# Attention heads worked off between the q and k panels of a two-stack transformer kernel

## The chip, the cores and the metric

The kernel is one launch on one core of a Trainium2 chip. The metric is the time of one execution on the device, in microseconds (us). The engines are TensorE (PE in the profile, with its weight loads as PEld), VectorE (DVE), ScalarE (ACT), GpSimd (POOL) and SyncE (SP), which issues the DMAs. Each engine works off its own list of instructions strictly in order, and a wait on a semaphore holds up everything behind it on that engine.

## The reference

The input is a stream of 256 tokens of width 1024. Two layers of a first stack, each with a convolutional feed-forward network (FFN) of inner width 2816, are followed by a second, larger block (a state-space branch, two attention-like branches and a mixture of 32 experts), whose norms are modulated by a vector that comes out of a small product with the "ada" weights. The change touches only the second layer of the first stack and its neighbours:

```
h = rms_norm(x, odd_norm_g)
q, k, v = split(h @ w_qkv)            # 16 heads of 64
q, k = rotary(q), rotary(k)
o = dilated_attention(q, k, v)        # 3 patterns, softmax over their log-sum-exps
x = x + o @ w_o
x = x + (silu(gate) * val) @ w_down   # the second FFN, gate and val from conv(rms_norm(x) @ w_up)
```

With 256 tokens the attention comes down to two blocks of 128 queries: for a head, 128 queries against 128 keys and 128 queries against 256 keys, with a bias that holds the mask and the weights of the patterns; then exp, a division by the sum, and the product with v.

## The kernel before, in words

Activations lie transposed, features on partitions and tokens along the free axis (128x256 tiles). Weights come in panels of 128x1024 f32 (512 KB) through a ring of four slots. In the first stack a panel is split into a rounded part `w_hi` (ACT, L1210 and L1216) and a remainder `w_lo` (DVE at L1559; GpSimd at L1530 for every fourth panel, slot 3), and one product is three matmuls: w_hi with r_hi (L598), w_hi with r_lo (L599), w_lo with r_hi (L600). A panel of eight input tiles is thus 24 matmuls into one of the four PSUM banks `lin[b]`. SyncE reloads a slot once it is split, so panels are loaded and split up to four ahead; ACT takes the rounded part of panel n+4 right after it took the result of panel n.

The second layer runs like this.

**Projection to q, k and v.** PE goes through 24 panels: q (8), k (8), v (8). After each of the 16 q and k panels ACT copies the result to `qs1` (L1255), and PE multiplies it by a permutation that swaps the halves of a head (`swap_halves`, L799, one matmul that goes in after the next panel). DVE multiplies by cos (L1759), the swapped one by sin (L1761), adds the two (L1762) and then makes `w_lo` of a later panel. The v panels are only copied.

**Attention.** After all 24 panels PE transposes v (16 transposes, L815, in four groups of which DVE copies each, L1769). Then a loop over 16 heads, skewed over the engines: in step i PE makes the scores of head i (L826, L827, into one half of `mixp`), after every second head one eighth of the third modulation row (L732), transposes the probabilities of head i-2 (L837, into one of two banks of `stat`), and multiplies the transposed probabilities of head i-3 by v (L846 to L848). DVE reads the scores and adds the bias (L1778), takes the maxima (L1782), and for the head before takes reciprocals (L1787) and scales (L1789); every second step it splits the output of a pair of heads into r_hi and r_lo (L1576, L1577). ACT makes exp (L1352) and copies the transposed probabilities (L1360):

```
if g >= 2:
    pe.wait_ge(pt_copied, g - 1)      # before the transposes of head g
```

**Behind it.** PE waits for the last pair of heads (`o_copied`), turns the modulation row into columns (`modulation_columns`, L741), waits until DVE has read them (`mod_read`), and goes on with the 8 panels of the output projection and with the FFN. The first FFN has two such groups of columns turned in the middle of its down projection.

**DMA order.** SyncE issues three ada loads of 1 MB ahead of the 24 panels, and the last five behind the fourth panel of the output projection; the ring for ada has three slots, so load a waits until PE has used row a-3 (L494), and the other four panels of the projection are queued behind these loads:

```
load_panels(3 * KD)
load_panels(4)
load_ada(5)
load_panels(KD - 4)
```

Of the kernel before, what the change touches and what calls it, by code (L numbers as in the profile page):

```python
# [29 lines left out]
P = 128  # L30
T = 256
# [147 lines left out]
def program(nc, A, out):  # L179
# [3 lines left out]
    with ctx:  # L183
# [263 lines left out]

        def downbank(n):

            return statbank(n) if n < 2 else mixbank(n)  # L450
# [119 lines left out]
        def _(pe):  # L570
# [99 lines left out]
            def ffn(modulated=False):  # L670
# [14 lines left out]
                if modulated:  # L685
                    pe.wait_ge(modrow_ready, 2)
# [15 lines left out]
                if modulated:  # L702
# [87 lines left out]
            ffn(True)  # L790


            def swap_halves(n):

                b = (qk_first + n) % 4
                pe.wait_ge(bank_free[b], panels.free[b])
                if n >= 2:
                    pe.wait_ge(qk_ready, n - 1)
                pe.matmul(stat[:, 2 * (n % 2), :], K["swap"], qs1[:, n % 2, :], start=True, stop=True)\  # L799
                    .then_inc(rot_ready, 1)  # L800

            qk_first = panels.n
            for n in range(16):
                linear(None, 1, first=n == 0)
                if n:
                    swap_halves(n - 1)
            linear(None, 1)
            swap_halves(15)
            linear(None, 7)
            panels.settled()  # L810
            for g in range(4):
# [6 lines left out]
            pe.wait_ge(vt1_copied, 4)  # L818
            pe.wait_ge(qk_ready, 16)
            for i in range(HEADS + 3):  # L820
                if i < HEADS:
# [7 lines left out]
                if i < HEADS and i % 2 == 1:  # L829
                    modulation(lin[2], 16 + i // 2, 1)  # L830
                if 2 <= i <= HEADS + 1:
                    g = i - 2
                    pe.wait_ge(probs_ready, g + 1)
                    if g >= 2:
                        pe.wait_ge(pt_copied, g - 1)
                    for c in range(3):
                        mm = pe.transpose(statbank(g)[:, c * P:(c + 1) * P], p1[:, g % 4, c * P:(c + 1) * P], K["ident"])  # L837
                    mm.then_inc(pt_ready, 1)
                if i >= 3:
                    g = i - 3  # L840
                    pe.wait_ge(pt_copied, g + 1)
                    if g >= 4 and g % 2 == 0:
                        pe.wait_ge(o_copied, g // 2 - 1)
                    o = lin[(g // 2) % 2][64 * (g % 2):64 * (g % 2) + 64, :]
# [5 lines left out]
            pe.wait_ge(o_copied, 8)  # L850
            modulation_columns(lin[2], 2)
            pe.wait_ge(mod_read, 3)
            project(None)
            ffn()
# [337 lines left out]
        def _(act):  # L1192
# [147 lines left out]
            for n in range(16):  # L1340
                if n >= 2:
                    act.wait_ge(qk_ready, n - 1)
                take(qs1[:, n % 2, :])
            for n in range(8):
                take(v1[:, n, :])
            for i in range(HEADS + 2):
                if i < HEADS:
# [7 lines left out]
                if i >= 2:  # L1355
# [4 lines left out]
                    act.activation(pt1[:, g % 4, :], statbank(g)[:, 0:SC], ACT.Copy).then_inc(pt_copied, 1)  # L1360
                    if i == HEADS:
                        split_hi(OUT1 + 1)
# [172 lines left out]
        def _(dve):  # L1535
# [61 lines left out]
            def ffn(l):  # L1597
# [57 lines left out]
                if l == 0:  # L1655
                    modulations(lin[0], 0)
                    modulations(lin[1], 1)
                for b in range(4):
# [97 lines left out]
            for n in range(16):  # L1756
                panels.taken(0)
                panels.advance(1)
                link(dve.tensor_tensor(rc1[:, 0, :], qs1[:, n % 2, :], K["cos"], ALU.mult))  # L1759
                dve.wait_ge(rot_ready, n + 1)  # L1760
# [501 lines left out]
```

## Time and profile before

| | us |
|---|---|
| median of 3 runs | 1676.15 (1671.21 to 1681.73) |
| profiled execution | 1676.46 |
| its span | 1674.7 |

| engine | busy, share of the span |
|---|---|
| PE | 1555.6 (93%) |
| PEld | 1269.1 (76%) |
| DVE | 691.7 (41%) |
| ACT | 511.4 (31%) |
| POOL | 117.7 (7%) |

The profiled execution is 0.3 us above the median. A busy time adds the time in which an engine had at least one instruction of its own under way. The ends of matmuls are modelled, so that PE is better read from the distance of the starts of two matmuls than from their lengths. In the timelines a row gives the start, the length, the engine, the line and the tiles; x8 is a number of instructions merged into a row; what stands in brackets is the idle time before it and what ended it. Two records with one line and one length next to each other belong to one f32 matmul, which PE takes in two.

### The profile page before, as it was taken

Reading aid. Unit: us, or ns where it says so; the run is one execution under the profiler, and the core shown is the slowest. Engines: PE = TensorE matmul, PEld = TensorE weight load, DVE = VectorE, ACT = ScalarE, POOL = GpSimd, SP = SyncE. Lnnn points to the kernel's source line nnn. Section 1 sums busy time; section 2 is a strip of 40 time slices with the busy share of each in tenths; the row PEclk is TensorE's granted clock in tenths of the full one; section 3 lists DMA queues with packets and bytes.
Section 4 is the critical chain, followed back from the end, with each engine's and each line's share of the span. In section 5 each row is a group of like instructions: output and inputs, shape, how many; then the busy total and the mean of one; then the engine's idle time right before and its main releaser. Section 6 shows DMA issues by size and latency. Waiting matters only on the chain.

```text
span 1674.7 us, 26947 instructions
## 1 busy us (share of the span) xinstructions
PE 1555.6 (93%) x10672; PEld 1269.1 (76%) x10672; DVE 691.7 (41%) x1296; ACT 511.4 (31%) x831; POOL 117.7 (7%) x50
## 2 busy tenths in 40 slices
PE   7988999989998999989998887998899999999997
PEld 5767999989678999978887876887666655555554
DVE  5945888357566886232414421412311111111111
ACT  2355554354446564352223104202111101111100
POOL 0111122212001122100000000000000000000000
PEclk9989999999999999989999987999799999999999
DMA  7664555745434656514442211354799999999994
GB/s 298 235 261 164 168 168 165 254 137 166 146 115 125 188 182 184 161 50 146 131 126 76 64 38 50 105 155 139 298 428 426 427 428 426 428 425 428 427 427 208
DMA packets 57977, 375.72 MB, mean 224 GB/s; under 512 B 6560, under 2 KB 6816, under 8 KB 42272
## 3 DMA queue, kind: packets, MB, share of 16 engines
q1 hardware_dynamic: 57888, 374.43, 60.6%
q8 instruction: 69, 1.13, 0.3%
q14 instruction: 20, 0.16, 0.0%
HBM read 373.35 MB, written 1.05 MB: 224 GB/s over the span
## 4 chain that ended last, share of the span: by engine, by line
PE 62%; DMA 15%; issue 12%; DVE 6%; ACT 3%; POOL 0%; SPq 0%; POOLq 0%; DVEq 0%; ACTq 0%
PE lin L617 15%; DMA moe_arena<-in_experts 14%; PE lin L598 5%; PE mixp L1145 4%; PE lin L599 4%; PE lin L600 4%; PE mixp L1149 4%; DVE mixers L1700 3%; PE lin L901 2%; PE stat L1169 2%; PE lin L1124 1%; PE stat L598 1%; PE mixp L600 1%; PE mixp L598 1%; PE stat L600 1%
## 5 line engine op out<-in xcount | busy, mean ns | idle before, releaser
L598 PE MATMUL lin<-r_hi,w_hi 128*128 128x256 f32 x1024 | 301.4, 294 | 16.8 <-DVE r_lo L1571 8.9
L599 PE MATMUL lin<-r_lo,w_hi 128*128 128x256 f32 x1024 | 293.7, 287 | 0.0
L600 PE MATMUL lin<-r_hi,w_lo 128*128 128x256 f32 x1024 | 293.6, 287 | 0.0
L617 PE MATMUL lin<-h,ring 128*128 128x256 f32 x1280 | 288.0, 385 | 3.0 <-DVE h L1583 3.0
L617 PEld LDWEIGHTS lin<-h,ring 128*128 128x128 f32 x1280 | 245.8, 193 | 40.7 <-issue 6.9
L598 PEld LDWEIGHTS lin<-r_hi,w_hi 128*128 128x128 f32 x1024 | 200.3, 196 | 22.9 <-issue 9.6
L599 PEld LDWEIGHTS lin<-r_lo,w_hi 128*128 128x128 f32 x1024 | 200.9, 196 | 0.7
L600 PEld LDWEIGHTS lin<-r_hi,w_lo 128*128 128x128 f32 x1024 | 200.5, 196 | 0.0
L1559 DVE TENSOR_TENSOR w_lo<-ring,w_hi 128x1024 fp32r<-128x1024 f32 x126 | 156.0, 1242 | 93.6 <-ACT w_hi L1216 70.1
L2175 DVE TENSOR_TENSOR moe_arena<-moe_arena,mixp 128x256 f32<-128x256 f32 x32 | 13.5, 421 | 353.3 <-ACT moe_arena L1505 353.3
L1216 ACT ACTIVATE w_hi<-ring 128x1024 fp32r<-128x1024 f32 x124 | 130.0, 1050 | 59.8 <-PE mixp L600 54.5
L1530 POOL TENSOR_TENSOR w_lo<-ring,w_hi 128x1024 fp32r<-128x1024 f32 x42 | 106.7, 2541 | 495.7 <-ACT w_hi L1216 299.3
L1169 PE MATMUL stat<-moe_arena 128*64 128x512 f32 x512 | 116.9, 598 | 0.0
L1145 PE MATMUL mixp<-moe_arena,h 128*64 128x256 f32 x512 | 77.6, 381 | 10.8 <-DMA moe_arena<-in_experts 10.8
L1145 PE MATMUL mixp<-moe_arena,cat 128*64 128x256 f32 x512 | 77.7, 381 | 5.2 <-DMA moe_arena<-in_experts 4.3
L1505 ACT ACTIVATE moe_arena<-mixp 128x256 f32<-128x256 f32 x32 | 12.3, 384 | 221.5 <-PE mixp L1149 221.5
L1169 PEld LDWEIGHTS stat<-moe_arena 128*64 128x64 f32 x512 | 33.9, 136 | 59.1 <-issue 54.8
L1149 PE MATMUL mixp<-moe_arena,cat 128*64 128x256 f32 x512 | 77.2, 379 | 0.0
L1149 PE MATMUL mixp<-moe_arena,h 128*64 128x256 f32 x512 | 77.0, 379 | 0.0
L1124 PE MATMUL lin<-moe_arena 64*128 64x256 f32 x528 | 65.9, 389 | 1.4 <-ACT moe_arena L1509 1.4
L1145 PEld LDWEIGHTS mixp<-moe_arena,h 128*64 128x64 f32 x512 | 35.7, 137 | 39.8 <-DMA moe_arena<-in_experts 21.3
L1262 ACT ACTIVATE ub<-lin,colp 128x256 f32<-128x256 f32 x88 | 49.3, 560 | 47.8 <-PE lin L600 47.8
(378 smaller groups left out, 2332.3 us busy)
## 6 DMA issues: line engine op xcount, KB each, us to landing
moe_arena<-in_experts SPq DMA_DIRECT2D x96, 2048.0 KB, 18.5
ring<-in_panels SPq DMA_DIRECT2D x272, 512.0 KB, 3.6
aring<-in_ada SPq DMA_DIRECT2D x24, 1024.0 KB, 6.3
cst<-in_consts SPq DMA_DIRECT2D x1, 1696.0 KB, 11.7
x<-in_x SPq DMA_DIRECT2D x1, 1024.0 KB, 4.7
out_x<-x SPq DMA_DIRECT2D x2, 512.0 KB, 2.6
mixers<-in_even_w_s SPq DMA_DIRECT2D x1, 512.0 KB, 13.4
colp<-in_cols SPq DMA_DIRECT2D x1, 361.5 KB, 5.1
```

The lines of the kernel that those rows point to most:

```text
L598: pe.matmul(o, w_hi[:, slot, c], r[0], start=start, stop=False, skip_group_check=True)
L599: pe.matmul(o, w_hi[:, slot, c], r[1], start=False, stop=False, skip_group_check=True)
L600: return pe.matmul(o, w_lo[:, slot, c], r[0], start=False, stop=stop, skip_group_check=True)
L617: mm = pe.matmul(lin[b][:, 0:T], w[:, i, :], rhs[:, i, :], start=i == 0, stop=i == k - 1)
L1124: mm = pe.matmul(lin[m // 2][:, (m % 2) * T:(m % 2 + 1) * T], e_yb[64 * half:64 * half + 64, j * P:(j + 1) * P], e_dT[64 * half:64 * half ...
L1145: pe.matmul(o[:, 0:T], lhs, e_wg[:, slot, k, half * T:(half + 1) * T], start=k == 0, stop=k == KD - 1, skip_group_check=True)
L1149: mm = pe.matmul(o[:, T:2 * T], lhs, e_wu[:, slot, k, half * T:(half + 1) * T], start=False, stop=k == KD - 1, skip_group_check=True)
L1169: mm = pe.matmul(statbank(1)[64 * half:64 * half + 64, :], e_hidT[:, k % 2, k // 2, :], e_wd[:, slot, k, half * 512:(half + 1) * 512], sta ...
L1216: act.activation(w_hi[:, n % RING, :], ring[:, n % RING, :], ACT.Copy).then_inc(w_hi_ready, 1)
L1530: pool.tensor_tensor(w_lo[:, POOL_SLOT, :], ring[:, POOL_SLOT, :], w_hi[:, POOL_SLOT, :].bitcast(F32), ALU.subtract).then_inc(w_split_pool, 1)
L1559: dve.tensor_tensor(w_lo[:, n % RING, :], ring[:, n % RING, :], w_hi[:, n % RING, :].bitcast(F32), ALU.subtract)\
L1700: ins = dve.scalar_tensor_tensor(cv0[:, j, :], hc0[:, j, tap:tap + T], w, cv0[:, j, :], ALU.mult, ALU.add)
```

## The change

1. The order of the panels in the weight stream is v (8), then q0, k0, q1, k1, ... (16).
2. PE projects v, then q0; transposes two groups of v; projects k0; transposes the other two. From then on each panel is followed by the swap of the panel before it and by one step of the head loop: `head(2n-3)` after panel 2n, `head(2n-2)` after panel 2n+1. Steps up to 12 go between panels. Steps 13 to 18 come behind the last panel.
3. The swapped product lies in the second half of the panel's own bank `lin[b]`; the transposed probabilities have one bank only (`statbank(0)`), so the transposes of head g wait for the copy of head g-1; the outputs of the heads lie in `stat[:, 2:4]`.
4. All eight parts of the modulation row stand behind the last panel: one after each of steps 13 to 18, two behind step 18. PE then waits for ACT's copy of the row (`modrow_ready`) and for all r_lo (`r_split`) ahead of the output projection.
5. The head outputs are copied to `h` by DVE; from the 13th step on ACT rounds them (`round_heads`) and DVE takes the remainder (`lower_heads`), instead of both by DVE out of PSUM at once.
6. The columns of the third group are turned within the down projection of the second FFN, and DVE reads them there.

```diff
-            def ffn(modulated=False):
+            def ffn(chunks):
...
-                if modulated:
-                    for chunk in range(2):
-                        pe.wait_ge(bank_free[chunk], panels.free[chunk])
-                        modulation_columns(lin[chunk], chunk)
+                for chunk in chunks:
+                    pe.wait_ge(bank_free[chunk], panels.free[chunk])
+                    modulation_columns(lin[chunk], chunk)
...
+            linear(None, KD, first=True)
+            v_taken, qk_first = list(panels.free), panels.n
+
+            def qk_panel(m):
+
+                if m >= 4:
+                    pe.wait_ge(qk_ready, m - 3)
+                linear(None, 1)
+
+            def swap_halves(m):
+
+                b = (qk_first + m) % 4
+                pe.wait_ge(bank_free[b], v_taken[b] + m // 4 + 1)
+                pe.matmul(swapped(b), K["swap"], qs1[:, m % 2, :], start=True, stop=True, skip_group_check=True)\
                     .then_inc(rot_ready, 1)
...
-            pe.wait_ge(vt1_copied, 4)
-            pe.wait_ge(qk_ready, 16)
-            for i in range(HEADS + 3):
-                if i < HEADS:
+            def head(i):
+
+                if 0 <= i < HEADS:
+                    pe.wait_ge(qk_ready, 2 * (i // 2) + 2)
+                    pe.wait_ge(vt1_copied, 4)
...
-                if i < HEADS and i % 2 == 1:
-                    modulation(lin[2], 16 + i // 2, 1)
...
-                    if g >= 2:
-                        pe.wait_ge(pt_copied, g - 1)
+                    if g:
+                        pe.wait_ge(pt_copied, g)
...
+            for n in range(8):
+                qk_panel(2 * n)
+                if n:
+                    swap_halves(2 * n - 1)
+                    head(2 * n - 3)
+                else:
+                    turn_values(0)
+                    turn_values(1)
+                qk_panel(2 * n + 1)
+                swap_halves(2 * n)
+                if n:
+                    head(2 * n - 2)
+                else:
+                    turn_values(2)
+                    turn_values(3)
+            swap_halves(15)
+            pe.wait_ge(qk_ready, 15)
+            panels.settled()
+            for i in range(13, HEADS + 3):
+                head(i)
+                modulation(lin[2], 16 + (i - 13), 1)
+            modulation(lin[2], 22, 2)
+            pe.wait_ge(modrow_ready, 3)
+            pe.wait_ge(r_split, 1 + KH + KD)
             project(None)
-            ffn()
+            ffn((2,))
...
# ACT
+            for n in range(8):
+                take_qk(2 * n)
+                if n:
+                    head(2 * n - 3)
+                take_qk(2 * n + 1)
+                if n:
+                    head(2 * n - 2)
+            def round_heads(first, last):
+
+                act.wait_ge(panel_done, panels.n)
+                for j in range(first, last):
+                    act.wait_ge(o_copied, j + 1)
+                    act.activation(r_hi[:, j, :], h[:, j, :], ACT.Copy).then_inc(r_hi_ready, 1)
+
+            for i in range(13, HEADS + 2):
+                head(i)
+                round_heads(max(i - 11, 0) if i > 13 else 0, i - 10)
+            round_heads(7, KD)
...
# DVE
-                    split_rows(j, lin[j % 2][:, 0:T]).then_inc(o_copied, 1)
+                    dve.tensor_copy(h[:, j, :], headbank(j)).then_inc(o_copied, 1)
...
+            for n in range(8):
+                if n:
+                    rotate(2 * n - 1)
+                    head(2 * n - 3)
...
+                rotate(2 * n)
+                if n:
+                    head(2 * n - 2)
+            rotate(15)
+            def lower_heads(first, last):
+
+                for j in range(first, last):
+                    dve.wait_ge(r_hi_ready, seen(r_hi_ready))
+                    dve.tensor_tensor(r_lo[:, j, :], h[:, j, :], r_hi[:, j, :].bitcast(F32), ALU.subtract).then_inc(r_split, 1)
+
+            for i in range(13, HEADS + 3):
+                head(i)
+                if i >= 14:
+                    lower_heads(i - 12 if i > 14 else 0, i - 11)
+            split_lo(OUT1 + 2)
+            lower_heads(7, KD)
```

`rotate(m)` on DVE is what the loop over n did before for a panel: cos, sin, add, and `w_lo` of the panel four on. `take_qk(m)` on ACT is the copy of a panel's result and `w_hi` of the panel four on.

## Rows read from the trace of the kernel before

**Rows 1.** The page: busy time, share of the span and instructions of each engine.

```profile
PE 1555.6 (93%) x10672; PEld 1269.1 (76%) x10672; DVE 691.7 (41%) x1296; ACT 511.4 (31%) x831; POOL 117.7 (7%) x50
```

**Rows 2.** Windows: stretch, its length, busy time of each engine, PEclk, DMA share, GB/s.

```profile
353.90:432.77 78.87, 78.78 (x608) 77.65 (x608) 52.97 (x77) 34.76 (x54) 17.49 (x6) 0.96 0.48 148
432.77:484.39 51.62, 46.23 (x297) 26.99 (x297) 40.27 (x121) 23.78 (x83) 0.00 (x0) 0.97 0.34 116
441.00:443.00 2.00, 2.00 (x10) 0.79 (x12) 1.82 (x7) 1.24 (x5) 0.00 (x0) 0.64 0.86 365
443.00:446.00 3.00, 3.00 (x18) 1.28 (x11) 1.28 (x6) 1.60 (x6) 0.00 (x0) 0.67 0.20 36
```

**Rows 3.** Timeline of PE: first transposes of v, first transposes of probabilities.

```profile
433.20 1.06 PE L815 MATMUL mixp<-cst,mixers 128*128 128x128 f32 x8 [0.52 <-issue]
440.67 0.55 PE L837 MATMUL stat<-cst,mixers 128*128 128x128 f32 x3 [1.24 <-DVE mixers L1789]
```

**Rows 4.** Timeline of PE: parts of the head loop and one ada part.

```profile
462.44 0.55 PE L837 MATMUL stat<-cst,mixers 128*128 128x128 f32 x3
462.92 0.43 PE L846 MATMUL lin<-mixers 128*64 128x128 f32 x2
463.72 0.48 PE L826 MATMUL mixp<-mixers 64*128 64x128 f32 x2
464.57 1.07 PE L732 MATMUL lin<-aring,c_act 128*32 128x512 f32 x8
465.57 0.55 PE L837 MATMUL stat<-cst,mixers 128*128 128x128 f32 x3
```

**Rows 5.** Timeline of PE, two groups of columns amid the first FFN's down projection.

```profile
332.80 1.84 PE L741 MATMUL lin<-cst,modrow 128*128 128x4 f32 x16
334.50 0.36 PE L598 MATMUL stat<-hid_hi,w_hi 128*128 128x256 f32 x1
```

**Rows 6.** Timeline of PE: first matmul of the output projection, two later ones.

```profile
484.39 0.39 PE L598 MATMUL lin<-r_hi,w_hi 128*128 128x256 f32 x1 [1.30 <-DVE mod L1672]
487.20 0.41 PE L598 MATMUL lin<-r_hi,w_hi 128*128 128x256 f32 x1
487.41 0.41 PE L599 MATMUL lin<-r_lo,w_hi 128*128 128x256 f32 x1
```

**Rows 7.** Timeline of PE, a swap between two panels.

```profile
411.95 0.59 PE L799 MATMUL stat<-mixers,cst 128*128 128x256 f32 x2
412.49 0.28 PE L599 MATMUL lin<-r_lo,w_hi 128*128 128x256 f32 x1
```

**Rows 8.** w_lo by DVE, whole kernel: count, ns min/median/max.

```profile
L1559 DVE TENSOR_TENSOR w_lo<-ring,w_hi x126: 1210/1222/3471, 112.9 to 697.4; 128x1024 fp32r<-128x1024 f32 x126
```

**Rows 9.** Timeline of DVE and ACT in one step of the head loop.

```profile
462.55 0.56 DVE L1778 SCALAR_TENSOR_TENSOR mixers<-mixp,cst 128x384 f32<-128x384 f32 x1 [0.82 <-PE mixp L827]
463.14 0.61 DVE L1782 TENSOR_REDUCE mixers<-mixers 128x1 f32<-128x128 f32 x2
463.79 0.40 ACT L1352 ACTIVATE mixers<-mixers 128x128 f32<-128x128 f32 x1 [1.33 <-DVE mixers L1782]
463.87 0.55 DVE L1789 TENSOR_SCALAR mixers<-mixers 128x128 f32<-128x128 f32 x2
464.33 0.42 DVE L1576 CAST r_hi<-lin 128x256 fp32r<-128x256 f32 x1
464.69 0.47 ACT L1360 ACTIVATE mixers<-stat 128x384 f32<-128x384 f32 x1
```

**Rows 10.** DMA issues in 433 to 485: count, size, median us to landing.

```profile
aring<-in_ada SPq DMA_DIRECT2D x5, 1024.0 KB, 5.0
```

**Rows 11.** Timeline of ACT, the copy of the modulation row.

```profile
480.03 0.59 ACT L1308 ACTIVATE modrow<-lin 128x512 f32<-128x512 f32 x1
```

**Rows 12.** Timeline of POOL and DVE, w_lo of two panels beside each other.

```profile
364.05 2.40 POOL L1530 TENSOR_TENSOR w_lo<-ring,w_hi 128x1024 fp32r<-128x1024 f32 x1 [19.92 <-ACT w_hi L1210]
364.06 3.47 DVE L1559 TENSOR_TENSOR w_lo<-ring,w_hi 128x1024 fp32r<-128x1024 f32 x1
```

More of the change, by code:

```diff
@@ L789, in _, with turn_values @@
             modulation(mixbank(1), 11, 5)
[L790 to L799, printed above, removed]
-                    .then_inc(rot_ready, 1)
[L802 to L811, printed above, removed]
+            ffn((0, 1))
+            linear(None, KD, first=True)
[8 more added lines that the diff above has]
+                pe.matmul(swapped(b), K["swap"], qs1[:, m % 2, :], start=True, stop=True, skip_group_check=True)\
+                    .then_inc(rot_ready, 1)
+            def turn_values(g):
+                for b in range(4):
+                    pe.wait_ge(bank_free[b], v_taken[b])
                 if g >= 2:
@@ L1339, in _, with take_qk, head @@
             stream_norm(down=True)
[L1340 to L1343, printed above, removed]
             for n in range(8):
                 take(v1[:, n, :])
-            for i in range(HEADS + 2):
-                if i < HEADS:
+            def take_qk(m):
+                if m >= 2:
+                    act.wait_ge(qk_ready, m - 1)
+                take(qs1[:, m % 2, :])
+            def head(i):
+                if 0 <= i < HEADS:
                     act.wait_ge(max_ready, i + 1)
@@ L1755, in _ @@
             split_lo(panels.n + 4)
[L1756 to L1760, printed above, removed]
-                link(dve.tensor_tensor(rc1[:, 1, :], stat[:, 2 * (n % 2), :], K["sin"], ALU.mult))
-                dve.tensor_tensor(qk1[:, n, :], rc1[:, 0, :], rc1[:, 1, :], ALU.add).then_inc(qk_ready, 1)
-                dve.wait_ge(qk_ready, n + 1)
-                split_lo(panels.n + 4)
-            panels.advance(8)
-            split_lo(panels.n)
-            for g in range(4):
-                dve.wait_ge(vt1_ready, g + 1)
-                dve.tensor_copy(vt1[:, g // 2, (g % 2) * 512:(g % 2 + 1) * 512], mixbank(g)).then_inc(vt1_copied, 1)
+            panels.advance(KD)
+            qk_first = panels.n
             a0 = list(K).index("bias00")
@@ L1772, in _, with rotate, head @@
             bias = cst[:, bias_at:bias_at + SC]
-            for i in range(HEADS + 3):
-                if i < HEADS:
+            def rotate(m):
+                panels.taken(0)
+                panels.advance(1)
+                link(dve.tensor_tensor(rc1[:, 0, :], qs1[:, m % 2, :], K["cos"], ALU.mult))
+                dve.wait_ge(rot_ready, m + 1)
+                link(dve.tensor_tensor(rc1[:, 1, :], swapped((qk_first + m) % 4), K["sin"], ALU.mult))
+                dve.tensor_tensor(qk1[:, 8 * (m % 2) + m // 2, :], rc1[:, 0, :], rc1[:, 1, :], ALU.add).then_inc(qk_ready, 1)
+                dve.wait_ge(qk_ready, m + 1)
+                split_lo(panels.n + 4)
+            def head(i):
+                if 0 <= i < HEADS:
                     dve.wait_ge(scores_ready, i + 1)
```

45 lines of the change are left out of this document (25 added, 20 removed).

## The prediction

> **What bounds the kernel now.** I read the page first: PE is busy 93% of the span, DVE 41%, ACT 31% [rows 1]. So work that leaves DVE or ACT is worth nothing by itself; only time in which PE stands still, or runs at a lower clock, can be won. Next I cut out the stretch that the change rearranges, with the windows [rows 2]: from the first matmul of the q, k, v projection at 353.90 to the first of the output projection at 484.39, 130.49 us in two parts. In the first part, 78.87 us, PE is busy for 78.78: nothing to win. The second part, the attention, is 51.62 us. The timeline tells what of it is PE's own work. Eight transposes of v take 1.06 [rows 3], 16 take 2.1. A step of the head loop, start to start, is 0.48 for the transposes, 0.80 for the product with v and 0.85 for the scores, 2.13 together; an ada part between steps adds 464.57 to 465.57, 1.00 [rows 4]. There the parts follow each other with no gap, so in mid-loop PE is the bound in the attention too. The sum is 2.1 + 16 x 2.13 + 8 x 1.00 + 0.85 for the columns (half of 332.80 to 334.50 [rows 5]) = 45.0. So 6.6 us of 51.62 is lost: waits like 0.52 and 1.24 [rows 3] and 1.30 [rows 6], and 5 us at a granted clock of 0.64 and 0.67 [rows 2], which is 2 x 0.36 + 3 x 0.33 = 1.7 us. **6.6 us, or 0.4% of the kernel, is the most that the rearrangement can win** in this stretch; the change takes no matmul away.
>
> **Part 1, panels reordered, v first.** The same 24 panels, swaps, w_hi and w_lo. The panels of the weight stream change places, not size or number. 0 (bounds 0 and 0: 78.78 of 78.87 was busy, and v panels need only a copy).
>
> **Part 2, heads between panels.** Steps up to 12 move between panels. I play one half period, from the end of a panel at 0. A panel is 24 matmuls at 0.12, 2.9 us; a swap put between panels costs 412.49 - 411.95 - 0.12 = 0.42 [rows 7]; a step 2.13; together 5.4 us for PE. PE: swap at 0, scores done at 1.2, transposes and product with v done at 2.5, next panel until 5.4, next swap and scores until 6.6, then the next transposes. DVE: sin and add, two 128x256 operations like the cast of 0.42, until 1.4; w_lo 1.22 [rows 8] until 2.6; read of the scores 0.59 until 3.2; maxima 0.53 until 3.7 (0.73 with the reciprocal, 0.2, taken off); reciprocal and scale 0.7 until 4.4; copy of an output until 4.9 [rows 9]. ACT: exp 0.90 from 3.8 to 4.7, copy of the transposed probabilities 0.47 until 5.2 [rows 9]. The next transposes want this copy, as there is one bank for them now, and PE is there at 6.6. The copy is 1.4 us early, the scaled probabilities 2.2. The cover for this is the panel of 2.9 us; without it PE would wait 1.5 us a step. So no wait between panels. What is added is a change of matmul kind: swap and head stand together, and the swap's 0.42 holds the change back to w_hi already, so another change costs between 0 and 0.42 for each of 13 insertions, nearer to 0; I take 0.09, **+1.2 us** (0 to 5.5).
>
> **Part 3, what is left behind the last panel.** Steps 13 to 18 have no panel to hide behind, only an ada part of 1.0 each. The clock starts at the end of the last panel. PE: step 12 until 2.5, last swap 2.8, scores of 13 at 3.6. The copy it needs is that of step 12, 5.2 by the schedule above: **waits 1.7**. Transposes, product, ada part until 7.6, scores of 14 at 8.5. DVE meanwhile: step 12 until 4.9, cos, sin, add until 6.2, w_lo until 7.4, read and maxima of 13 until 8.5; ACT exp and copy until 10.0: PE **waits 1.5**. Step 14 with its ada part ends at 12.4, scores of 15 at 13.2. ACT rounds three outputs until 11.3 and is done with step 14 at 12.7. DVE, held by the remainders of three outputs (3 x 0.42), has the maxima of 15 at 14.4, ACT's copy is at 15.9, and PE, done with step 15 at 15.5, **waits 0.5**. The rest goes at PE's pace: step 16 ends at 18.3, 17 at 20.6, 18 at 22.4.
>
> Then the ada rows. Before, the eight parts were 5 us apart; now they stand 2 to 5 us apart with two at the end. The ring holds three, so the load of part 22 is issued when PE is done with 19 (18.3), that of 23 when it is done with 20 (20.6). Landing takes 5.0 us [rows 10]: 23.3 and 25.6. PE is there at 22.4 and 24.3: **waits 0.9 and 1.3**, and ends at 26.6. Then ACT copies the row, 0.59 [rows 11], with 0.2 around it, and PE, now told to wait for it, **waits 0.8**: the output projection starts at 27.4. On SyncE the last four panels of the projection are queued behind these loads, as before; they are issued at 20.6, and PE wants the first of them four panels after 27.4. Nobody is late by that.
>
> Waits: 1.7 + 1.5 + 0.5 + 0.9 + 1.3 + 0.8 = 6.7 us. The granted clock fell once before, behind the waits at the start of the head loop, for 1.7 us; the same kind of waits stand at the start of this tail, so I take 1.7 again (0 to 3.4: never, or twice). Both together 8.4, against 6.6 before: **+1.8 us**. The low end, with the waits of the tail gone, is -6.6; the high end, with each wait twice as long, +8.5.
>
> **Part 4, modulation columns.** Out of the stretch come 0.85 of work (its waits are in the 6.6). They reappear within the down projection of the second FFN for 0.85 and a change of kind: net 0 to 0.2. DVE's reads there have a whole down projection beside them: 0. The projection's first matmuls ran at 0.21 apart around 487.20 instead of 0.12 [rows 6]; the wait ahead of it stays of like size, so this stays.
>
> **Part 5, outputs through h.** The operations on the outputs go from two on DVE to two on DVE and one on ACT, off PE's path except for the 0.5 above.
>
> **Sum.** 0 + 1.2 + 1.8 + 0.1 = +3.1 us on the profiled execution of 1676.46, which stands 0.3 above the median of 1676.15: 1679.3 from the median, **1679 us**. A measurement of this kernel can hardly tell less than 1% (17 us) from no change; its three runs lie 10 us apart. This is no change.
>
> **Rivals.**
>
> *The handover works.* If ACT and DVE keep ahead in the tail, because they have caught up during the last panel more than I count, and the ada loads land in time, the waits and the lower clock of the tail go: 3.1 - 8.4 = -5.3, 1671 us. For it: before, the loop ran at PE's pace with the same chain. Against it: there the transposes had two banks, and DVE now starts the tail with a rotation and a w_lo in front.
>
> *GpSimd holds DVE.* At 364.05 a w_lo on GpSimd of 2.40 us ran beside one on DVE that took 3.47 instead of 1.22, 2.25 more [rows 12]. In the panels with heads there are three of GpSimd's (behind the 6th, 10th and 14th q or k panel). Were DVE held for 2.25 right behind the scores, the copy would come 2.25 - 1.4 = 0.9 late: 3 x 0.9 = 2.7, 1682 us. It decides nothing near 1%. Against it: of that half period DVE does not make a w_lo itself. The Trainium skill (SBUF — State Buffer, "Who interferes with whom") calls the port pair of VectorE and GpSimd an exclusive lock, which whoever starts first has for a whole instruction. That agrees with the row of 3.47. By that rule the read of the scores, with one operand in PSUM, would go on beside GpSimd, and only the scale would be held; the scale has 2.2 us to spare by the schedule above, and this rival would cost nothing.
>
> *The clock falls between the panels* (the other side). The panels' stretch was granted 0.96 with only a 128x256 swap between panels; the heads' small matmuls and their waits brought stretches at 0.64 and 0.67 [rows 2]. At the lower clock of 1.2 GHz matmuls stand 0.21 instead of 0.12 apart [rows 6], so a panel costs 24 x 0.09 = 2.2 us more. Fourteen panels have heads about them: 14 x 2.2 = 30, 1710 us; from seven panels on (3 + 15) it is more than 1%. For it: the heads leave PE's array partly unused. Against it: in mid-loop the heads alone, with no wait, ran at full clock, and my schedule has no wait between the panels.
>
> *The order convoys*, so that each inserted step waits a little for DVE or ACT: half a us for each of 13 is 6.5, 1686 us. It would need the 1.4 us of slack above to be used up first.
>
> **How the numbers follow.** The forecast 0.58; the handover works 0.20; GpSimd 0.05; convoy 0.08; clock 0.07; something that speeds the kernel by over 1% 0.02, which no row offers: 6.6 us of lost time bound it. The low end of the range is the handover case, 1671; the high end takes in the convoy, 1688. Left out are the clock case and the tails of the others. Faster by over 1%: 0.02. Slower by over 1%: the clock case and a bit of a worse convoy, 0.08. Within 1%: 0.90.
>
> **What would show it.** PE without a gap between panels, a half period of 5.4 us, and the copy of the transposed probabilities over a us ahead of the next transposes; behind the last panel waits of one to two us on ACT's copies in steps 13 and 14, then on the ada DMAs of parts 22 and 23 (not there: the landing was faster, or the steps slower); 27 us from the end of the last panel to the output projection; 133 us for the whole stretch; four column matmuls within the second down projection. Wrong would be gaps between the panels, a granted clock under 0.9 there, or a tail under 20 us.

## The result, and the profile after

The changed kernel took 1686.49 us in the median of 7 runs (1680.71 to 1689.46), the kernel before 1676.64 (1671.19 to 1681.73): ratio 1.0063, 95% interval 1.0042 to 1.0084. It is slower by 0.4 to 0.8%, so within 1%, and 7.5 us above the time forecast. The profiled execution took 1686.49, its span is 1684.7, 10.0 above that of before. In the rows of the changed kernel L812 is the swap, L835 the scores, L844 the transposes, L853 the product with v, L738 an ada part, L747 the columns and L606 to L608 the three matmuls of a panel.

The windows cut the span of the changed kernel where those of before were cut: the part with the panels, what stands behind the last panel, and the stages between the end of the second FFN and the first expert load. Columns as in [rows 2].

```profile
354.03:461.00 106.97, 106.97 (x769) 94.47 (x769) 73.70 (x154) 51.37 (x113) 17.28 (x6) 0.97 0.35 109
461.00:488.23 27.23, 20.47 (x128) 8.70 (x127) 14.03 (x43) 9.46 (x31) 0.00 (x0) 0.89 0.67 249
...
711.21:1173.69 462.48, 423.25 (x2144) 371.71 (x2142) 140.88 (x243) 116.08 (x187) 0.00 (x0) 0.93 0.31 91
```

The stretch of [rows 2] was 130.49 us and is 134.20: +3.7. PE is busy for all of 106.97 in the panels' part, with heads between the panels, and for 20.47 of 27.23 behind it. From there to the end of the second FFN it was 222.03 and is 222.98, +0.95. The stages behind, which no line of the change touches, were this before:

```profile
706.42:1163.68 457.26, 417.65 (x2144) 366.80 (x2142) 140.81 (x243) 116.10 (x187) 0.00 (x0) 0.95 0.31 92
```

The same 2144 matmuls, DVE busy for 140.8 and ACT for 116.1 in both, yet 5.2 us more and a granted clock of 0.93 instead of 0.95. So of 10 us that the profile shows, 4.7 lie where the change is, and 5.2 where it is not. Neither figure is free of the clock: in the first ten microseconds of the output projection, for one, it was 0.78 here and 0.83 before.

**Between the panels**, the timeline of PE shows one half period, from swap to swap:

```profile
435.31 0.59 PE L812 MATMUL lin<-mixers,cst 128*128 128x256 f32 x2
435.83 0.48 PE L835 MATMUL mixp<-mixers 64*128 64x128 f32 x2
436.68 0.55 PE L844 MATMUL stat<-cst,mixers 128*128 128x128 f32 x3
437.16 0.43 PE L853 MATMUL stat<-mixers 128*64 128x128 f32 x2
...
440.93 0.59 PE L812 MATMUL lin<-mixers,cst 128*128 128x256 f32 x2
```

No row carries a bracket, so nothing was waited for. The parts of a step stand 0.85 and 0.48 apart as in [rows 4], but the period is 5.62, where a panel with a swap (24 x 0.12 + 0.42) and a step (2.13) make 5.43. The swap takes 0.52 until the scores. The copies that the transposes need were early, as forecast: the one before the transposes of 442.31 ends at 440.67, 1.6 us ahead. GpSimd held DVE there, at no cost to PE: beside its w_lo the scale took 1.39 us instead of 0.55:

```profile
425.72 3.45 POOL L1580 TENSOR_TENSOR w_lo<-ring,w_hi 128x1024 fp32r<-128x1024 f32 x1 [18.06 <-ACT w_hi L1239]
428.13 1.39 DVE L1847 TENSOR_SCALAR mixers<-mixers 128x128 f32<-128x128 f32 x2
```

**Behind the last panel** (the swap after it starts at 457.80), the timeline of PE at each wait:

```profile
463.30 0.52 PE L844 MATMUL stat<-cst,mixers 128*128 128x128 f32 x3 [1.30 <-ACT mixers L1393]
467.91 0.52 PE L844 MATMUL stat<-cst,mixers 128*128 128x128 f32 x3 [1.45 <-ACT mixers L1393]
475.44 0.52 PE L844 MATMUL stat<-cst,mixers 128*128 128x128 f32 x3 [0.51 <-ACT mixers L1393]
482.64 1.06 PE L738 MATMUL lin<-aring,c_act 128*32 128x512 f32 x8 [0.82 <-DMA aring<-in_ada]
485.68 1.86 PE L738 MATMUL lin<-aring,c_act 128*32 128x512 f32 x8 [1.98 <-DMA aring<-in_ada]
488.23 0.58 PE L606 MATMUL lin<-r_hi,w_hi 128*128 128x256 f32 x1 [0.70 <-ACT modrow L1337]
```

Three waits for ACT's copy of transposed probabilities, two for the last ada loads, one for the copy of the row: 6.8 us. The row of 485.68 lasts 1.86 instead of 1.07 [rows 4]: the lower clock. From the end of the last panel to the output projection it is 30.4 us, where the schedule had 27.4 and the clock's 1.7 beside it.

What stands ahead of ACT's copies is seen in the timeline of DVE and ACT:

```profile
462.69 0.47 ACT L1393 ACTIVATE mixers<-stat 128x384 f32<-128x384 f32 x1
464.03 1.22 DVE L1609 TENSOR_TENSOR w_lo<-ring,w_hi 128x1024 fp32r<-128x1024 f32 x1
465.18 0.55 DVE L1836 SCALAR_TENSOR_TENSOR mixers<-mixp,cst 128x384 f32<-128x384 f32 x1
466.41 0.40 ACT L1385 ACTIVATE mixers<-mixers 128x128 f32<-128x128 f32 x1 [3.25 <-DVE mixers L1840]
467.30 0.47 ACT L1393 ACTIVATE mixers<-stat 128x384 f32<-128x384 f32 x1
```

The scores of step 13 were done by 462.0, but DVE rotates the last panel and makes a w_lo first, reads them at 465.18, and ACT, idle for 3.25, comes to the copy at 467.30, for which PE waits until 467.91.

**In the second FFN** the columns stand where they were put, and 703.67 - 702.87 = 0.80 goes to them (with the change of kind behind them 0.9):

```profile
702.87 0.95 PE L747 MATMUL lin<-cst,modrow 128*128 128x4 f32 x8
703.67 0.36 PE L606 MATMUL stat<-hid_hi,w_hi 128*128 128x256 f32 x1
```

### The profile page after: what moved, and what is told of

It is laid out like the page before. It is cut to its first block, busy times and chain, and to the rows that moved or that the text cites. A ratio compares the mean times of both kernels' runs of the same rounds, so it can differ in the third digit from the quotient of the medians.

```text
span 1684.7 us, 26972 instructions
## 1 busy us (share of the span) xinstructions
PE 1564.5 (93%) x10672; PEld 1273.2 (76%) x10672; DVE 692.8 (41%) x1296; ACT 512.3 (30%) x839; POOL 117.4 (7%) x50
## 3 DMA queue, kind: packets, MB, share of 16 engines
HBM read 373.35 MB, written 1.05 MB: 222 GB/s over the span
## 4 chain that ended last, share of the span: by engine, by line
PE 62%; DMA 15%; issue 12%; DVE 6%; ACT 4%; POOL 0%; SPq 0%; POOLq 0%; DVEq 0%; ACTq 0%
PE lin L625 14%; DMA moe_arena<-in_experts 14%; PE lin L606 5%; PE mixp L1174 4%; PE lin L607 4%; PE lin L608 4%; PE mixp L1178 4%; DVE mixers L1757 3%; PE lin L930 2%; PE stat L1198 2%; PE lin L1153 1%; PE stat L606 1%; PE mixp L608 1%; PE mixp L606 1%; PE stat L607 1%
## 5 line engine op out<-in xcount | busy, mean ns | idle before, releaser
L606 PE MATMUL lin<-r_hi,w_hi 128*128 128x256 f32 x1024 | 300.0, 293 | 16.3 <-DVE r_lo L1621 8.9
L608 PE MATMUL lin<-r_hi,w_lo 128*128 128x256 f32 x1024 | 293.2, 286 | 0.0
L606 PEld LDWEIGHTS lin<-r_hi,w_hi 128*128 128x128 f32 x1024 | 200.0, 195 | 25.8 <-issue 11.8
L608 PEld LDWEIGHTS lin<-r_hi,w_lo 128*128 128x128 f32 x1024 | 200.6, 196 | 0.0
L1153 PEld LDWEIGHTS lin<-moe_arena 64*128 64x128 f32 x528 | 48.4, 186 | 18.6 <-issue 12.3
```

The lines of the kernel that those rows point to most:

```text
L606: pe.matmul(o, w_hi[:, slot, c], r[0], start=start, stop=False, skip_group_check=True)
L608: return pe.matmul(o, w_lo[:, slot, c], r[0], start=False, stop=stop, skip_group_check=True)
L1153: mm = pe.matmul(lin[m // 2][:, (m % 2) * T:(m % 2 + 1) * T], e_yb[64 * half:64 * half + 64, j * P:(j + 1) * P], e_dT[64 * half:64 * half ...
```

## The experiments

Medians and ratios are against runs of the kernel before on the same chip. Its median was 1678.28 in the first series (18 runs), 1678.71 in the second (35) and 1676.33 in the third (17). The first series has before_late_5, before_late_2, tail_fill and columns_back, the second before_again, after_again, before_columns and tail_best, the third the other four; before and after are the runs of the result.

| kernel | median | ratio (95%) | stretch | to the end of FFN 2 | stages behind |
|---|---|---|---|---|---|
| before | 1676.64 | 1 | 130.49 | 222.03 | 457.26 |
| before_again | 1678.66 | 1.0005 (0.9988, 1.0023) | 130.56 | 219.76 | 459.63 |
| before_columns | 1675.66 | 0.9994 (0.9978, 1.0009) | 128.23 | 220.47 | 461.34 |
| before_late_2 | 1682.37 | 1.0030 (1.0009, 1.0052) | 130.46 | 224.66 | 461.39 |
| before_late_5 | 1688.08 | 1.0064 (1.0046, 1.0082) | 134.96 | 229.74 | 461.58 |
| before_late_5_again | 1686.10 | 1.0051 (1.0031, 1.0072) | 130.63 | 228.22 | 461.52 |
| before_late_7 | 1692.58 | 1.0076 (1.0049, 1.0103) | 134.98 | 233.21 | 458.26 |
| after | 1686.49 | 1.0063 (1.0042, 1.0084) | 134.20 | 222.98 | 462.48 |
| after_again | 1686.79 | 1.0047 (1.0029, 1.0065) | 134.13 | 223.13 | 462.54 |
| columns_back | 1684.52 | 1.0044 (1.0028, 1.0060) | 136.78 | 222.68 | 456.97 |
| after_late_2 | 1689.31 | 1.0065 (1.0044, 1.0086) | 134.92 | 226.85 | 457.13 |
| tail_fill | 1682.13 | 1.0039 (1.0011, 1.0067) | 131.03 | 220.47 | 458.08 |
| tail_best | 1675.39 | 0.9990 (0.9976, 1.0005) | 126.1 | 223.5 | 458.55 |
| tail_best_2 | 1674.79 | 0.9985 (0.9974, 0.9997) | 125.2 | 222.7 | 457.38 |

The last three columns come from the one profile of each kernel: from the first q, k, v matmul to the first of the output projection, from there to the first residual addition behind the second FFN, from there to the first expert load. The last two kernels have 2 us of ada work behind the start of the projection.

### A shift by other means

```diff
+                if not modulated:
+                    pe.wait_ge(bank_free[2], panels.free[2])
+                    for r in range(6):
+                        for i in range(4):
+                            pe.matmul(lin[2][:, 4 * i:4 * i + 4], modrow[:, 0, i * P:(i + 1) * P], K["ident"][:, 0:P:32],
+                                      start=True, stop=True, skip_group_check=True)
                 for k in range(18, KF - 2):
```

> The kernel before, with six groups of four column matmuls without use (0.85 us a group) put into the down projection of the second FFN: 5.1 us of PE work more, ahead of the stages that neither kernel changes. Theory A (clock episodes move with the program): the stages from the end of the second FFN to the first expert load were 457.2 us before and 462.4 after the change, with the same instructions, because all of them start 4.8 us later and the stretches at the lower clock fall on other work; a shift of 5.1 by other means then gives 462 too, and the total is up 10 (1687). Theory B (the changed program itself slows these stages): they stay at 457 and the total is up 5 (1682).

> The same with three groups, 2.55 us. Theory A: the later stages take anything from 455 to 463 us, not in proportion to the shift. Theory B: 457, and the total is up 2.5.

 (The edit with 3 rounds instead of 6.)

The medians rose by 10 and 4. Taken alone they speak for theory A. But the profile of before_late_5 lost 4.5 us already in the head loop, 250 us ahead of the first added instruction:

```profile
452.20 1.94 PE L738 MATMUL lin<-aring,c_act 128*32 128x512 f32 x8
...
434.00:456.00 22.00, 19.63 (x90) 10.20 (x89) 13.19 (x39) 7.65 (x28) 0.00 (x0) 0.69 0.31 103
```

The same window of before, with the same instructions in the same order:

```profile
434.00:456.00 22.00, 19.63 (x121) 10.26 (x120) 16.84 (x52) 9.09 (x35) 0.00 (x0) 0.92 0.41 144
```

PE was busy for 19.63 us in both and started 121 matmuls in one and 90 in the other. The granted clock fell behind the same wait, and came back after less than 5 us in the one (0.64 over two microseconds and 0.67 over three [rows 2]) and after some 14 in the other, where ada parts took 1.94 instead of 1.07 as late as 452.20. That is no effect of the program, which is the same up to there: here the drop begins behind the same wait, but its length is drawn anew in each execution.

And the probe is not clean. The second FFN took 7.7 us more than before for what was meant as 5.1 us of added work. The 24 column matmuls stand from 702.91 to 708.91, which is 6.0; the clock fell within them and stayed down behind them:

```profile
706.00:716.00 10.00, 10.00 (x61) 10.00 (x62) 0.00 (x0) 0.00 (x0) 0.59 (x1) 0.66 0.17 56
```

### The clock: is the loss behind the second FFN drawn or caused?

> The kernel before, unchanged, once more. Theory A in its second form (the lower clock comes and goes in time of its own, and how much of each disturbed stage it takes is drawn anew in each execution): this profile has the same instructions in the same order, yet the stages from the end of the second FFN to the first expert load may take anything from 457 to 462.5 us and the head loop 51 to 56; its times spread over 10 us and its median is the one of before. Rival (the lower clock is a fixed function of the program): the profile repeats that of before within 0.5 us in each stage, 130.5, 222.0, 457.3.

> The changed kernel, unchanged, once more. What the change itself costs is then the difference of medians over many runs: by the two stretches it touches 3.7 + 0.95 = 4.7 us, ratio 1.003, if the 5.2 us behind the second FFN were drawn (theory A, second form); 10 us, ratio 1.006, if they belong to the change. The stretch to the output projection repeats at 132 to 136 us by either.

Neither kernel has an edit. The windows behind the second FFN, of before_again:

```profile
703.15:1162.78 459.63, 420.05 (x2144) 369.47 (x2142) 140.87 (x243) 115.99 (x187) 0.00 (x0) 0.94 0.30 92
```

and of after_again:

```profile
711.63:1174.17 462.54, 423.31 (x2144) 371.71 (x2142) 140.82 (x243) 116.03 (x187) 0.00 (x0) 0.93 0.30 91
```

The fixed function is out: before_again has 2.4 us more here than before, and 2.3 less in the stage ahead, where the output projection ran without the drop of [rows 6], as the first ten microseconds of that stage show, of before:

```profile
484.39:494.50 10.11, 10.11 (x72) 10.11 (x73) 2.38 (x5) 2.73 (x4) 0.67 (x1) 0.83 0.53 183
```

and of before_again:

```profile
483.39:493.50 10.11, 10.11 (x82) 10.06 (x83) 2.71 (x6) 3.46 (x6) 1.98 (x1) 1.00 0.56 192
```

Over all fourteen profiles these stages took 457.0 to 462.5 us with the same matmuls; in the nine read this way a longer one has a lower granted clock, 0.95 at 457 and 0.93 from 461 on. The Trainium skill (TensorE: Matmul & The Clock Gate, "What's actually happening") says that the gate looks at activity on a beat that does not start with the kernel, so that the same kernel comes out differently from run to run; the two windows of the head loop above agree in that: the same instructions, 0.92 and 0.69.

Where the 5.2 us arise can be read by setting the two profiles against each other, instruction for instruction. Counted from the start of these stages, the changed kernel is 1.6 us behind after 35 us and 5.2 behind from DVE's instruction at 990.4 on (1000.4 in the changed kernel), and most of the 3.6 between comes in the few microseconds ahead of it. One instruction of PE there, before, and the next of its line:

```profile
984.44 1.09 PE L1020 MATMUL mixp<-arena 128*64 128x128 f32 x8 [0.85 <-DVE arena L2022]
991.55 1.97 PE L1020 MATMUL mixp<-arena 128*64 128x128 f32 x8 [1.30 <-DVE arena L2019]
```

and the first of them in the changed kernel:

```profile
990.83 1.86 PE L1049 MATMUL mixp<-arena 128*64 128x128 f32 x8 [0.85 <-DVE arena L2099]
```

The wait ahead is 0.85 us in both. Before, the clock was still up behind it and fell two waits later; in the changed kernel it fell behind this one. That is no effect of the change, since before_again, with no edit, has the early drop too (1.80 us for that row, at 979.80). So in a row of waits it is also drawn at which of them a drop begins.

But the changed kernel had 462.5 twice, and its ratio 1.0047 (1.0029 to 1.0065) over 12 more runs is 4.9 to 10.9 us, which leaves out 4.7, though barely. So chance alone does not cover it.

The granted clock that each run has on record tells more than two profiles. Its mean is 0.9611 over the 19 runs of the changed kernel and 0.9644 over 82 runs of before from the three series, 0.0033 less, give or take 0.0011 (95%); within the second series alone it is 0.9612 (12 runs) against 0.9643 (35). So the changed kernel does run at a lower clock on average. Over those 82 runs an execution is 1.1 us shorter for each 0.001 that its clock is higher. By that estimate 3.7 us of the 8.4 between the means of the two kernels are the clock's, and 4.7, give or take 1, are there at an equal clock. In tail_best and tail_best_2 below, which differ from the changed kernel in the tail and the first two panels behind it alone, the mean clock is 0.9657 and 0.9666 (12 runs each): it is the order of the tail that costs the clock. Some of it falls in the tail itself; how much falls in later stages, and why, is open.

Three more kernels asked whether the time follows a beat in the shift:

> The kernel before, with eight groups of useless column matmuls in the second FFN, 6.8 us. So far a shift of 2.55 cost 5 us in the median and one of 5.1 cost 10.7 (7.7 to 13.7). If the lower clock follows a beat of its own, against which the shift moves the later stages, the cost beyond the shift is not in proportion: at 6.8 it may be back to nothing, total 7 to 9, less than at 5.1. If a shift simply costs double (each us late costs another), the total is 13.6. If the excess was chance, 6.8.

> The shift of 5.1 once more on the same chip as the one of 6.8. Beat: again 8 to 11 us over before. Chance: 5.1, with the stages behind the second FFN anywhere from 457 to 462.5 in the profile.

> The changed kernel, with three groups of useless column matmuls in the second FFN, 2.55 us. Two profiles of the changed kernel had 462.5 us behind the second FFN; the one with the columns back, which gets there 2.2 us later, had 457.0. Beat: 2.55 us later than the changed kernel, these stages take 457 to 459, and the total is 2 to 3 us under the changed kernel though it does more. Chance or a cost of the program itself: 2.5 over it, 1689.

```diff
+                if 2 in chunks:
+                    pe.wait_ge(bank_free[3], panels.free[3])
+                    for r in range(3):
+                        for i in range(4):
+                            pe.matmul(lin[3][:, 4 * i:4 * i + 4], modrow[:, 0, i * P:(i + 1) * P], K["ident"][:, 0:P:32],
...
```

The beat's forecasts missed, but for the repeat of 5.1 (8 to 11 us, 9.8 came): 6.8 us of work cost 1.0076 (8 to 17 us) and was not back to nothing, and after_late_2 was 2.8 us above the changed kernel, not 2 to 3 under it, though its profile had the short form of the later stages, 457.13. Forecast of a price of double was 13.6 for the 6.8, and 12.7 came; but most of the double price is the probe's own: in the profiles 5.1 us of added work made the FFN 7.7 and 6.2 longer, 6.8 made it 11.2. With that, the ratios of the shifted kernels hold no excess that is clear of their intervals. What stays is this: in a single profile up to 5.5 us of the later stages are drawn, so the repeated 462.5 proves nothing by itself; that the changed kernel has the lower clock on average is shown by its 19 runs, and a beat in the shift, of which two of three forecasts missed, does not explain it.

### Part 4 alone, and undone

```diff
-            modulation_columns(lin[2], 2)
-            pe.wait_ge(mod_read, 3)
+            pe.wait_ge(modrow_ready, 3)
             project(None)
-            ffn()
+            ffn((2,))
...
```

> The kernel before with part 4 of the change alone: the third group of columns is turned amid the second FFN. Out of the stretch go 0.85 us of matmuls and waits of up to 1.3, into the FFN come 0.95: the stretch 128.2, the FFN 223, the sum 1.2 us shorter. By medians hardly to be told from before. If the columns' new place cost more than that, the FFN would be above 223.5.

The stretch came to 128.23, forecast 128.2. The stage to the end of the second FFN came to 220.47, not 223: in this profile, as in before_again, the output projection started at full clock (1.00 over its first ten microseconds). Against before_again the two stages together are 1.6 us shorter, forecast 1.2. The ratio, 0.9994 (0.9978 to 1.0009), cannot tell a gain of that size.

```diff
-            pe.wait_ge(modrow_ready, 3)
+            modulation_columns(lin[2], 2)
+            pe.wait_ge(mod_read, 3)
             pe.wait_ge(r_split, 1 + KH + KD)
             project(None)
-            ffn((2,))
+            ffn(())
...
```

> The changed kernel with part 4 undone: the third group of columns is turned right ahead of the output projection again, which waits for DVE's reading. Both theories of the stretch: the projection starts 0.85 for the matmuls and 1.3 for the wait later, 2.2 us, and the second FFN is 0.95 shorter; so the end of the second FFN comes 1.2 us later than in the changed kernel. Theory A for the stages behind: anything from 455 to 463 us. Theory B: 462, as in the changed kernel.

The stretch grew by 2.6, forecast 2.2, and the end of the second FFN came at 713.40, 2.2 later than in the changed kernel, forecast 1.2: the drop behind the last ada wait now also covers the columns, 1.87 instead of 1.05. Behind it the profile is among the short ones (456.97), so that this span is 3.5 us shorter than the changed kernel's with the same work in it. The ratios of the two kernels, 1.0044 and 1.0047, have intervals that overlap. Moving the columns is right and by the profiles worth one to two microseconds; it is not the loss.

### The tail: filled, then rearranged

```diff
+                if i >= 13:
+                    modulation(lin[2], 16 + (i - 13), 1)
                 if 2 <= i <= HEADS + 1:
...
                 head(i)
-                modulation(lin[2], 16 + (i - 13), 1)
```

> The changed kernel, with the ada part of each of the steps 13 to 18 put between the scores and the transposes of the step instead of behind it, so that it covers the wait for ACT's copy. Theory (the tail is a chain of waits that PE sits out): waits of 1.3 and 1.45 us in steps 13 and 14 fall by up to 1.0 each, that of 0.5 in step 16 goes; the loads of the last ada parts are issued that much earlier; the stretch to the output projection falls from 134.2 to about 131, to 129 if the granted clock stays up. Rival (the tail is bound by the DVE and ACT chain): the waits stay in sum and the stretch stays within 0.7 us of 134.2.

The waits of PE in the tail, in total, times, longest:

```profile
PE lin L738 <- DMA aring<-in_ada: 3.3, 3, 1.4
PE stat L846 <- ACT mixers L1394: 1.8, 2, 1.5
PE lin L606 <- ACT modrow L1338: 0.7, 1, 0.7
```

The stretch was 131.03; forecast was 131, and 129 if the clock stayed up. It did stay up, 1.00 behind the panels, so by that the time came out 2 us too long. The waits for ACT fell from 3.3 to 1.8; that for the loads rose from 2.8 to 3.3, since the parts now follow each other faster than loads of 5 us land in a ring of three. The wait of 1.45 in step 14, forecast to fall by up to 1.0, did not move at all.

```diff
-            modulation(lin[2], 22, 2)
-            pe.wait_ge(modrow_ready, 3)
             pe.wait_ge(r_split, 1 + KH + KD)
-            project(None)
+            for m in range(KD):
+                if m == 2:
+                    pe.wait_ge(modrow_ready, 3)
+                linear(None, 1)
+                if m == 0:
+                    modulation(lin[0], 22, 2)
+                if m >= 2:
+                    stream_sum([m - 2])
+            for m in (KD - 2, KD - 1):
+                stream_sum([m])
```

Beside this the ada parts of steps 13 to 18 stand between scores and transposes, as in tail_fill, and all eight go into the bank lin[0].

> The changed kernel, with the ada part of steps 13 to 18 between scores and transposes, in bank lin[0] instead of lin[2], and the last two parts behind the first panel of the output projection instead of ahead of it; PE waits for the copy of the row only ahead of the third panel. Theory (the last waits on ada loads and on the row's copy are exposed for their place alone): in the last kernel 1.03 and 1.42 for loads and 0.7 for the copy go; the output projection starts at about 127 us of the stretch, with 2 us of ada work behind it; from the first q, k, v matmul to the end of the second FFN 349 us against 357 of the changed kernel and 352.5 before; the median 3 us under before. Rival (the time is lost in the panels' part, by 0.2 us a step): the tail gains nothing that the median shows, and this kernel stays 3 us or more above before.

The projection starts at 479.71, 126.1 us from the start of the stretch, with no wait for a load or the row:

```profile
PE stat L846 <- ACT mixers L1401: 1.8, 2, 1.5
PE lin L606 <- DVE r_lo L1880: 1.5, 1, 1.5
```

To the end of the second FFN it is 349.7, against 357.2 in the changed kernel, 352.5 before and 350.3 in before_again. The median fell by 11 us from that of after_again, taken on the same chip, of which these 7.5 can be placed in the profiles. Nothing but the ada parts, their bank and the wait for the row was changed, so it is the order of the tail that made the changed kernel slow. Against the kernel before, the ratio 0.9990 (0.9976 to 1.0005) is no gain yet.

```diff
                 dve.wait_ge(qk_ready, m + 1)
-                split_lo(panels.n + 4)
+                if m < 15:
+                    split_lo(panels.n + 4)
```

This comes on top of the edits of tail_best.

> The changed kernel with the rearranged ada parts (as in the last but one series) and, on DVE, w_lo of the last panel taken out of the rotation of the last k panel, so that the read of step 13's scores is not behind it. Theory: the wait of 1.45 us in step 14 is DVE's w_lo of 1.2; it falls to 0.3, the output projection starts at 125 us of the stretch instead of 126.3; median some 1 us under that kernel, 4 under before. Rival: another wait (exp, or the product's o) takes its place and the stretch stays at 126.3.

The timeline of PE in steps 13 and 14:

```profile
467.45 0.52 PE L846 MATMUL stat<-cst,mixers 128*128 128x128 f32 x3 [0.30 <-ACT mixers L1401]
470.93 0.52 PE L846 MATMUL stat<-cst,mixers 128*128 128x128 f32 x3 [0.31 <-ACT mixers L1401]
```

1.45 has become 0.31: the wait was DVE's w_lo of 1.2 ahead of the read of the scores, passed on by ACT. The stretch fell by 0.9, forecast 1.3, to 125.2. With a ratio of 0.9985 (0.9974 to 0.9997) this kernel beats the one before, by 0.5 to 4.4 us, and the changed one by some 12. What it gains on tail_best, 0.6 us by medians of different series, the runs cannot tell from nothing.

## Why the prediction was right or wrong

**The bound.** Right in kind. PE was the bound, 6.6 us were put as the most to be had, and the rearrangement did not win them. The 6.6 are 0.5 too low: eight transposes of v were priced at the modelled length of their row, 1.06, but in the changed kernel the panel behind them starts 0.79 after them (382.65 to 383.44), so the 16 are 1.6 and not 2.1.

**Part 2, no wait between the panels.** Right: 106.97 of 106.97 busy, and the copy 1.6 us early against 1.4 forecast. The price of an insertion was put too low: 5.62 - 5.43 = 0.19 a step against 0.09, so 2.5 us for 13 instead of 1.2. The swap's 0.42 did not cover the change to the scores; between swap and scores 0.52 passes.

**Part 3, the tail.** The schedule of waits held to a degree that one cannot count on: 1.7, 1.5, 0.5, 0.9, 1.3 and 0.8 were forecast, 1.30, 1.45, 0.51, 0.82, 1.98 and 0.70 came, 6.8 in sum against 6.7. That the sum is so close is in part luck, as the first came 0.4 shorter and the fifth 0.7 longer. The mis-sized term is the clock's, taken at 1.7 us: by the same reckoning 27.23 us at 0.89 are 3.0, because a second drop came with the last ada wait. By the starts of PE's rows, which leave out the time that PE was idle anyway, it is 2.4: 1.6 in step 14 and 0.8 in the last ada part. tail_best shows what this tail costs for its order alone: with waits for loads and row gone and the scores' wait filled, 7.5 us less in the same two stages.

**Part 4.** Right: 0.80 for the columns in the FFN by the timeline, and 2.3 out of the stretch with the wait (before_columns). That the stage grew by 0.95, just as forecast, is partly luck, as the clock at the start of the projection differed too. The wait had been counted in the 6.6, where part 3's new wait of 0.70 took its place.

**The sum.** +3.1 forecast, +3.7 + 0.95 = +4.7 measured in the two stages. The 1.6 between them are 1.3 from the insertions, 0.7 from the clock (2.4 for 1.7) and 0.1 from the waits, less the 0.5 by which the idle time of before was put too low.

**What the sum left out.** It held the 1,000 us behind the change constant. In the profile they were 5.2 longer, by the granted clock alone. One profile against another can draw some 4 us of that: the profile of before had a short form of these stages, 457.26, where the median of the seven profiles of kernels built on before is 461.34. But the medians are 9.9 us apart too, and 8.1 in the second series, and by the 19 and 82 runs some 3.7 us are a lower clock that comes with the changed kernel. The forecast allowed the clock a cost in the tail and, as a rival, between the panels, and none behind them. That 1686.5 is still inside the range, which reached to 1688, is luck in this: the range got there by the convoy's price, and there was no convoy.

**The rivals.** The handover did not work by itself; it mostly does with the ada parts and one w_lo moved (tail_best_2, 1674.79 where this rival had 1671). A stall by GpSimd and a convoy would both show as waits of PE between the panels, and there are none. GpSimd did hold DVE there: beside a w_lo of GpSimd the scales at 406.63, 428.13 and 450.62 took 1.38 or 1.39 us instead of 0.55, within what they had to spare, while the reads of the scores at 426.82 and 449.32 kept their 0.55. The clock did not fall between the panels: it was 0.97 there, with the one drop at the start that [rows 2] has too.

## What to carry to other kernels

Work put between other work of the bound engine costs its change of kind (here 0.19 us each), and what it saves is only the idle time it fills; count that first, and then draw up the schedule of what is left at the end, since there the waits that were hidden come out again. Fill such a tail with independent work ahead of the waiting instruction, not behind it, and keep loads that a small ring gates away from its last microseconds. Before a difference of a few microseconds in a profile is explained, look at stages that both kernels have alike: here 5 of 10 us were in them.

## What the runs showed of the hardware

- TensorE's granted clock fell to half behind a wait, but where and for how long differed between executions of the same instructions: behind the same wait of the head loop it was down for less than 5 us in one and some 14 in another (434 to 456: 0.92 and 0.69), and behind a wait of 0.85 near 985 it fell in one and stayed up in another. Stages with equal instructions took 457.0 to 462.5 us.
- In one kernel the time of an execution goes with its mean granted clock: 1.1 us shorter for each 0.001 more, over 82 runs of before (the changed kernel 0.9611 over 19 runs, tail_best 0.9657 over 12).
- Column matmuls with four columns, 24 or 32 in a row with no wait, brought a drop of their own, which began within them: 0.66 over 706 to 716 in before_late_5, where 24 of them end at 708.91. Behind four (the changed kernel) and behind twelve (before_late_2) there was none, behind 16 (after_late_2) 0.83 over 706 to 716.
- Beside a w_lo of GpSimd, DVE's scale (two 128x128 operations) took 1.39 us instead of 0.55, and its read of the scores out of PSUM the usual 0.55 (changed kernel, 426 to 452).
- The swap between two panels costs 0.42 us, its own work included; ahead of the scores, 64 rows deep, it holds PE for 0.52.
